# Moving the low-half subtractions of 32 quarters from VectorE to GpSimd in a decoder block

## The chip, the core and the metric

One core of a Trainium2 chip runs the whole kernel. The metric is the device time of one execution in microseconds (us). The engines are named as the profile names them: PE is TensorE's matmul, PEld its weight load, DVE is VectorE, ACT is ScalarE, POOL is GpSimd, SP is SyncE, which here only issues DMAs.

## What is computed

A decoder block over 1024 tokens of width 1024, in float32: attention with a sliding window beside a convolution, then an expert layer. This case is about the expert layer, which takes more than the last two thirds of the time:

```
q = (xb @ w_q).reshape(T, PEER_HEADS, 2, PEER_QDIM // 2)
s = jnp.einsum('thpc,hpkc->thpk', q, sub_keys)
top_s, top_i = lax.top_k(s, PEER_TOPK)
cand = top_s[:, :, 0, :, None] + top_s[:, :, 1, None, :]
best_s, best_c = lax.top_k(cand.reshape(T, PEER_HEADS, PEER_TOPK * PEER_TOPK), PEER_TOPK)
ids = i1 * N_KEYS + i2
g = jax.nn.softmax(best_s, axis=-1)
ue, ve = u_tab[ids], v_tab[ids]
act = gelu(einsum('td,thkd->thk', xb, ue))
out = einsum('td' <- 'thk,thkd', g * act, ve)
```

Each token picks 128 of 16384 experts (8 heads of 16). U and V (`u_tab`, `v_tab`) are 16384 x 1024 each.

## The kernel before, in words

The expert layer splits the tokens in halves of four 128-token tiles. The **first product** multiplies the tokens of tiles 1 to 3 of the lower half with all rows of U and writes the results to DRAM (`hidden`), from which the picked ones are read later; those of tile 0 are made one by one, as **dots** of a token with its gathered rows of U. A **second stage** treats the upper half densely (x times U, gelu, gates, times V) while the picked rows of V are gathered and summed for the lower half.

The first product runs over 128 **quarters**. Four quarters are a block of 512 experts; a quarter is two of the eight 128-row slices of the contraction. Float32 is made of two parts in the type fp32r, a high half that is the rounded value and a low half that is the rest. For each quarter Q:

- SP loads 512 KB of U into slot Q % 4 of `xraw` (`load_x`, L398), once the low half of quarter Q - 4 is made.
- ACT casts it to the high half `hx` (`high_u`, L822; the cast is L831), once TensorE has read the slot's old contents.
- The low half is `lx = xraw - hx`, one `tensor_tensor` of 128 x 1024 float32 (`low_wide`, L1237; L1240). Before the change VectorE makes all 128 of them.
- TensorE waits for the low half (L1793) and does 18 matmuls of 128 x 512 (L1801), six for each of three token tiles.
- After the fourth quarter of a block ACT copies three results to `hst` (`evict`, L854) and SP stores them (L417).

Around this, VectorE's program is one list in order (L1420 to L1434). At quarter Q it makes the low half first, then a share of the **picks**, then the marks, then the dots. The picks choose the 16 best experts per head of each of the eight token tiles, in 14 steps a tile (`pick`, L1250): sums of candidates (step 0), `max`, `max_index` and `match_replace` (steps 1 to 5), digits, ranks, 0/1 tables and their reductions (steps 6 to 13). Five tiles, 70 steps, are spread over quarters 4 to 35, 2.2 steps a quarter; the other three tiles over quarters 36 to 121. **Marks** (L1352) are 0/1 tables of 8 tokens of the upper half; from them POOL makes a scaled copy (`scale_hot`, L549) and ACT a plain one (L885), and TensorE multiplies the two in a **hot block** of 8 matmuls (L1787): two hot blocks in every three quarters from quarter 21 on. POOL's program (L595 to L601) does `scale_hot(n)` one quarter ahead of its hot block, and from quarter 39 on gathers the rows of U for the dots (L577; VectorE, L1409).

Three waits couple the engines besides: ACT takes the exponential of a tile's best scores (L858), in its own order behind the cast of a later quarter, and waits there for VectorE's step 6 (`best_ready`); TensorE transposes a tile's picks (L1777) after quarters 17, 24, 30 and 36 and waits for VectorE's step 13; step 10 on VectorE waits for the exponential.

Of the kernel before, what the change touches and what calls it, by code (L numbers as in the profile page):

```python
# [55 lines left out]
QB = DK // KQ  # L56
# [3 lines left out]
QUARTERS = QB * NB  # L60
FIRST_PICKS = 1 + HT
FIRST_QUARTERS = 36
LAST_PICK = QUARTERS - 6
X_BLOCK = FIRST_QUARTERS // QB - 1
X_QUARTER = FIRST_QUARTERS + 4
DOT_FROM = X_QUARTER + 1
# [15 lines left out]
VR = 2  # L82
# [30 lines left out]
F32 = mybir.dt.float32  # L113
# [3 lines left out]
ALU = mybir.AluOpType  # L117
# [5 lines left out]
def picks_done(Q):  # L123
    first = FIRST_PICKS * STEPS_PICK
    if Q < FIRST_QUARTERS:
        return first * max(0, Q + 1 - QB) // (FIRST_QUARTERS - QB)
    return min(NT * STEPS_PICK, first + (NT * STEPS_PICK - first) * (Q + 1 - FIRST_QUARTERS) // (LAST_PICK - FIRST_QUARTERS))


def query_place(m, half):  # L130

    return (1, 3, 2, 4)[2 * m + half] if m < 2 else 2 * m + half + 1


def quarter_of_step(k):
# [3 lines left out]
def stores(slot):  # L139
    return len(range(slot, (NB - 1) * PT, HSLOTS))  # L140
# [6 lines left out]
def hot_quarter(n):  # L147
    return 21 + n * 3 // 2
# [18 lines left out]
def decoder_block(nc, x, xT, w_in, w_out, w_q, keysT, uT, uX, u_tab, v_tab, ffn_g, consts, params, final_g, out):  # L167
# [15 lines left out]
    def at(offset, name, shape, dt=F32):  # L183

        with ExitStack() as there:
            if offset:
                there.enter_context(nc.sbuf_tensor(f"below_{name}", [P, offset // 4], F32))
            return there.enter_context(nc.sbuf_tensor(name, shape, dt))

    def sem(name):  # L190
        return ctx.enter_context(nc.semaphore(name))

    with ctx:
# [49 lines left out]
        xraw = at(HN, "xraw", [P, QB, KQ, WIDTH])  # L243
        hst = at(HN + 16384, "hst", [P, HSLOTS, WIDTH])
        hx = [at(offset, f"hx{r}", [P, KQ, WIDTH], F32R)
              for r, offset in enumerate((HN + 24576, HN + 28672, MID + 8192, MID + 12288))]
        lx = [at(MID + offset, f"lx{r}", [P, KQ, WIDTH], F32R)
              for r, offset in enumerate((82400, 86496, 123360, 127456))]
# [68 lines left out]
        def sems(names):  # L317
            return [sem(n) for n in names.split()]
# [16 lines left out]
        q_ready, q_copied, ks_ready, ks_free, wqh_ready, wql_ready = sems("q_ready q_copied ks_ready ks_free wqh_ready wql_ready")  # L335
        xraw_in = [sem(f"xraw_in{r}") for r in range(QB)]
        hx_ready, lx_ready, x_used, h1_ready, h1_free = sems("hx_ready lx_ready x_used h1_ready h1_free")
        hst_out = [sem(f"hst_out{n}") for n in range(HSLOTS)]
        best_ready, exp_ready, sel_ready, selT_ps, selT_ready = sems("best_ready exp_ready sel_ready selT_ps selT_ready")
        ids_ready = sem("ids_ready")  # L340
# [29 lines left out]
        def _(sp):  # L370
# [26 lines left out]

            def load_x(Q):  # L398
                if Q >= QB:
                    sp.wait_ge(lx_ready, Q - QB + 1)  # L400
                else:
                    sp.wait_ge(xl_ready, 2 * DK)
                b, r = divmod(Q, QB)
                sp.dma_start(xraw[:, r, :, :], uX[b, r]).then_inc(xraw_in[r], 16)

            def load_gates(g):
                sp.dma_start(gt[:, :, :, :], gates[g]).then_inc(g_in, 16)

            def store_hidden(B):
                for n in range(PT):  # L410
                    e = B * PT + n
                    sp.wait_ge(h1_free, e + 1)
                    dst = hidden[n * P:(n + 1) * P, B * WIDTH:(B + 1) * WIDTH]
                    if B == NB - 1:
                        sp.dma_start(dst, hlast[:, n, :]).then_inc(hlast_out, 16)
                    else:
                        sp.dma_start(dst, hst[:, e % HSLOTS, :]).then_inc(hst_out[e % HSLOTS], 16)  # L417
# [14 lines left out]
            for B in range(NB):  # L432
                for Q in range(QB * (B + 1) + 3, min(QB * (B + 2) + 3, QUARTERS)):
                    load_x(Q)
                if B == 0:
                    sp.dma_start(x_rows[0], xh[1][:, :, :].bitcast(F32)).then_inc(x_out, 16)
                    sp.dma_start(x_rows[1], xl[1][:, :, :].bitcast(F32)).then_inc(x_out, 16)
                if B == X_BLOCK:

                    sp.wait_ge(rows_out, 16)  # L440
                    sp.wait_ge(sel_ready, FIRST_PICKS)
                    sp.dma_start(uring[1][:, :], h_rows[:, 0, :]).then_inc(xt_in, 16)
                    sp.dma_start(uring[2][:, :], ffn_g.partition_broadcast(P)).then_inc(xt_in, 16)
                if B == NB - 1:
                    for c in range(2):
                        sp.wait_ge(lx_ready, QUARTERS - QB + c + 1)
                        sp.dma_start(u_raw[:, c, :], uT[c]).then_inc(u_in[c], 16)

                    for slot in range(HSLOTS):
                        sp.wait_ge(hst_out[slot], 16 * stores(slot))  # L450
                    load_gates(0)
                store_hidden(B)
                if B == hot_quarter(HT * BLOCKS - 1) // QB + 1:
                    for b in range(2):
                        sp.wait_ge(gates_out[b], 16 * (HALF // SUB // 2))
                    sp.wait_ge(hot_scaled, HT * BLOCKS + RAW)
                    sp.dma_start(xh[1][:, :, :].bitcast(F32), x_rows[0]).then_inc(x_back, 16)
                    sp.dma_start(xl[1][:, :, :].bitcast(F32), x_rows[1]).then_inc(x_back, 16)
                    sp.wait_ge(gp_ready, HT * BLOCKS * HQ + ROWS_CREDIT)
# [8 lines left out]
            def load_group(g, first=False):  # L468
                for c in range(GC):
                    n = g * GC + c  # L470
                    if n + 2 < NKEY:
                        sp.wait_ge(uh_ready, n + 1)
                        sp.wait_ge(ul_ready, n + 1)
                        sp.dma_start(u_raw[:, n % 2, :], uT[n + 2]).then_inc(u_in[n % 2], 16)
                    if not first or c >= VR:
                        sp.wait_ge(vh_ready, n - VR + 1)
                        sp.wait_ge(vl_ready, n - VR + 1)
                    sp.dma_start(v_raw[:, c % VR, :], v_tab[n]).then_inc(v_in[c], 16)
                    if c == 1 and not first:
                        sp.wait_ge(w_ready, g * GC)  # L480
                        load_gates(g)

            for c in range(VR):
                sp.wait_ge(lx_ready, QUARTERS - VR + c + 1)
            load_group(0, first=True)
            load_rows(1)
            load_rows(0)
# [11 lines left out]
        def _(pool):  # L499
# [91 lines left out]
                    in_offset=bass.IndirectOffsetOnAxis(ap=idsA[:, n, k:k + 1], axis=0)).then_inc(v_got[q % VS], 16)  # L591


            pool.sem_inc(hot_scaled, RAW)
            for Q in range(QUARTERS):  # L595
                for n in range(HT * BLOCKS):
                    if hot_quarter(n) - 1 == Q:
                        scale_hot(n)
                for k in range(P):
                    if quarter_of_dot(k) - 2 == Q:  # L600
                        gather_dot(k)  # L601
# [383 lines left out]
        def _(dve):  # L985
# [432 lines left out]

            marked = 0
            for Q in range(QUARTERS):  # L1420
                if Q >= QB:
                    low_wide(Q)
                picked(Q)
                if Q == X_QUARTER:
                    normed_rows()
                while marked < HT * BLOCKS and hot_quarter(marked) - 3 <= Q:
                    if marked == 0:
                        dve.drain()
                        dve.wait_ge(rows_out, 16)
                        dve.wait_ge(x_out, 32)  # L1430
                    mark(*divmod(marked, BLOCKS))
                    marked += 1
                for k in range(dots_done(Q - 1) if Q else 0, dots_done(Q)):
                    dot(k)  # L1434
# [55 lines left out]
        def _(pe):  # L1490
# [299 lines left out]

            def hidden_quarter(Q):
                B, quarter = divmod(Q, QB)
                pe.wait_ge(lx_ready, Q + 1)  # L1793
                for n in range(PT):
                    e, t0 = B * PT + n, (n + 1) * P
                    if quarter == 0 and e >= HSLOTS:
                        pe.wait_ge(h1_free, e - HSLOTS + 1)
                    for kk in range(KQ):
                        k = quarter * KQ + kk
                        for w, u in ((xh[0], hx), (xh[0], lx), (xl[0], hx)):  # L1800
                            last = mm(ps[:, e % HSLOTS, :], w[:, k, t0:t0 + P], u[quarter][:, kk, :],  # L1801
                                      start=k == 0 and w is xh[0] and u is hx, stop=k == DK - 1 and w is xl[0])
                    if quarter == QB - 1:
                        last.then_inc(h1_ready, 1)
                if quarter < QB - 1:
                    last.then_inc(x_used, 1)
                for n in range(HT * BLOCKS):
                    if hot_quarter(n) == Q:
                        hot_block(n)
# [130 lines left out]
```

## Time and profile before

| | us |
|---|---|
| median of 3 runs (lowest to highest) | 2835.77 (2834.06 to 2838.0) |
| profiled execution, whole | 2834.67 |
| its span, first to last instruction | 2832.7 |
| mean granted TensorE clock | 0.985 of full |

Busy shares of the span: PE 97%, DVE 80%, POOL 53%, ACT 37%. Busy time is that of instructions on an engine; a wait is the engine's idle time, put down to what ended it. In a timeline a row is start, duration, engine, line, operation, out<-in, shape and a count; the duration of a VectorE or GpSimd instruction runs from where the engine took it up to its end, so that neighbours can overlap by 0.1 us or so and a time in which the instruction could not get at its data is part of its duration.

### The profile page before, as it was taken

Reading aid. Unit: us, or ns where it says so; the run is one execution under the profiler, and the core shown is the slowest. Engines: PE = TensorE matmul, PEld = TensorE weight load, DVE = VectorE, ACT = ScalarE, POOL = GpSimd, SP = SyncE. Lnnn points to the kernel's source line nnn. Section 1 sums busy time; section 2 is a strip of 40 time slices with the busy share of each in tenths; the row PEclk is TensorE's granted clock in tenths of the full one; section 3 lists DMA queues with packets and bytes.
Section 4 is the critical chain, followed back from the end, with each engine's and each line's share of the span. In section 5 each row is a group of like instructions: output and inputs, shape, how many; then the busy total and the mean of one; then the engine's idle time right before and its main releaser. Section 6 shows DMA issues by size and latency. Waiting matters only on the chain.

```text
span 2832.7 us, 33409 instructions
## 1 busy us (share of the span) xinstructions
PE 2744.7 (97%) x11792; PEld 2098.8 (74%) x11792; DVE 2276.5 (80%) x3815; ACT 1034.6 (37%) x1374; POOL 1495.7 (53%) x1194
## 2 busy tenths in 40 slices
PE   8999699999899999999899999999999999999998
PEld 3444345888777888888778888888888888888886
DVE  1985533688998898888588889888989888898986
ACT  4443523211346656666323232232322323223233
POOL 3892100111023656665367777777777777777630
PEclk9989899999999999999999999999999999999999
DMA  5110100212546999999999898888989889888983
GB/s 194 45 45 1 60 15 23 75 46 84 203 149 220 323 329 345 335 348 344 373 358 330 300 328 306 314 315 306 327 298 327 301 312 327 301 326 299 342 302 137
DMA packets 254838, 687.75 MB, mean 243 GB/s; under 512 B 32080, under 2 KB 97744, under 8 KB 249168
## 3 DMA queue, kind: packets, MB, share of 16 engines
q0 software_dynamic: 104448, 335.81, 33.6%
q1 hardware_dynamic: 84432, 316.27, 30.9%
q10 hardware_dynamic: 65792, 33.56, 4.2%
q8 instruction: 93, 1.52, 0.2%
q14 instruction: 73, 0.60, 0.1%
HBM read 614.22 MB, written 71.30 MB: 242 GB/s over the span
## 4 chain that ended last, share of the span: by engine, by line
PE 71%; DVE 12%; DMA 7%; POOL 4%; DVEq 2%; issue 2%; ACT 1%; ACTq 0%; POOLq 0%; SPq 0%
PE ps L1836 24%; PE ps L1828 24%; PE ps L1801 6%; PE ps L1749 6%; DMA vring<-in_u_tab,idsA 5%; PE ps L1619 4%; DVE ps L1021 2%; POOL hnT L526 2%; PE ps L1787 1%; DVE lx L1240 1%; DVE vring L1409 1%; PE ps L1526 1%; POOL vring L577 1%; PE ps L1614 1%; DVE marks L1352 1%
## 5 line engine op out<-in xcount | busy, mean ns | idle before, releaser
L589 POOL DMA_INDIRECT vring<-in_v_tab,idsA x512 | 554.1, 1082 | 306.3 <-DVE ps L1392 162.7
L1392 DVE SCALAR_TENSOR_TENSOR ps<-vring,hsel,ps 128x1024 f32<-128x1024 f32 x508 | 652.7, 1285 | 29.4 <-DMA vring<-in_v_tab,idsA 11.7
L564 POOL DMA_INDIRECT hsel<-hidden,idsE x384 | 411.6, 1072 | 125.7 <-issue 106.4
L1836 PE MATMUL ps<-vh,wh 128*128 128x512 f32 x1024 | 401.9, 392 | 4.2 <-DVE acc L1469 4.2
L1836 PE MATMUL ps<-vh,wl 128*128 128x512 f32 x1024 | 405.9, 396 | 0.0
L1828 PE MATMUL ps<-xh,ul 128*128 128x512 f32 x1024 | 404.3, 395 | 0.0
L1828 PE MATMUL ps<-xh,uh 128*128 128x512 f32 x1024 | 403.4, 394 | 0.7 <-ACT hlast L854 0.7
L1828 PE MATMUL ps<-xl,uh 128*128 128x512 f32 x1024 | 402.4, 393 | 0.0
L1836 PE MATMUL ps<-vl,wh 128*128 128x512 f32 x1024 | 402.3, 393 | 0.0
L950 ACT CAST vh<-v_raw 128x1024 fp32r<-128x1024 f32 x128 | 134.1, 1047 | 585.5 <-PE ps L1836 580.0
L1801 PE MATMUL ps<-hx,xh 128*128 128x512 f32 x768 | 312.8, 407 | 29.0 <-DVE lx L1240 25.1
L1801 PE MATMUL ps<-lx,xh 128*128 128x512 f32 x768 | 308.7, 402 | 0.0
L1801 PE MATMUL ps<-hx,xl 128*128 128x512 f32 x768 | 306.9, 400 | 0.0
L577 POOL DMA_INDIRECT vring<-in_u_tab,idsA x128 | 181.1, 1414 | 161.9 <-DVE vring L1409 148.2
L549 POOL TENSOR_TENSOR hot<-marks,selG 128x1024 f32<-128x1024 bf16 x64 | 133.0, 2078 | 222.1 <-DVE marks L1352 127.3
L1836 PEld LDWEIGHTS ps<-vh,wh 128*128 128x128 f32 x1024 | 192.5, 188 | 49.1 <-DVE acc L1469 5.5
L831 ACT CAST hx<-xraw 128x1024 fp32r<-128x1024 f32 x128 | 134.1, 1049 | 256.7 <-PE ps L1801 166.1
L1836 PEld LDWEIGHTS ps<-vl,wh 128*128 128x128 f32 x1024 | 192.5, 188 | 47.0
L1828 PEld LDWEIGHTS ps<-xl,uh 128*128 128x128 f32 x1024 | 192.1, 188 | 46.3
L1828 PEld LDWEIGHTS ps<-xh,uh 128*128 128x128 f32 x1024 | 192.7, 188 | 45.0 <-ACT hlast L854 1.1
L1828 PEld LDWEIGHTS ps<-xh,ul 128*128 128x128 f32 x1024 | 192.3, 188 | 45.1
L1836 PEld LDWEIGHTS ps<-vh,wl 128*128 128x128 f32 x1024 | 192.4, 188 | 43.3
(197 smaller groups left out, 4707.6 us busy)
## 6 DMA issues: line engine op xcount, KB each, us to landing
xraw<-in_uX SPq DMA_DIRECT2D x128, 512.0 KB, 6.1
u_raw<-in_uT SPq DMA_DIRECT2D x128, 512.0 KB, 6.3
v_raw<-in_v_tab SPq DMA_DIRECT2D x128, 512.0 KB, 7.1
gates<-gbuf ACTq DMA_DIRECT2D x16, 2048.0 KB, 22.5
gt<-gates SPq DMA_DIRECT2D x32, 1024.0 KB, 9.0
hidden<-hst SPq DMA_DIRECT2D x93, 256.0 KB, 8.5
wbuf<-in_w_in SPq DMA_DIRECT2D x19, 512.0 KB, 3.6
wqbuf<-in_w_q SPq DMA_DIRECT2D x16, 512.0 KB, 3.5
```

The costliest lines, as they stand in the source:

```text
L549: nc.gpsimd.tensor_tensor(hot[:, b % ROWS, 1, :, :].rearrange("p (c e) k -> p c e k", e=2), marks[:, b % RAW, 1, :, :, :].rearrange("p c k ...
L564: nc.gpsimd.indirect_dma_start(out=hsel[:, n, k:k + 1], out_offset=None, in_=hidden_items, in_offset=bass.IndirectOffsetOnAxis(ap=idsE[:, ...
L577: nc.gpsimd.indirect_dma_start(out=uring[k % US][:, :], out_offset=None, in_=u_rows, in_offset=bass.IndirectOffsetOnAxis(ap=idsA[:, 0, k:k ...
L589: nc.gpsimd.indirect_dma_start(out=vring[q % VS][:, :], out_offset=None, in_=v_rows, in_offset=bass.IndirectOffsetOnAxis(ap=idsA[:, n, k:k ...
L831: nc.scalar.copy(hx[r][:, :, :], xraw[:, r, :, :]).then_inc(hx_ready, 1)
L950: nc.scalar.copy(vh[:, c, :], v_raw[:, c % VR, :]).then_inc(vh_ready, 1)
L1392: nc.vector.scalar_tensor_tensor(out=bank2(6), in0=vring[slot][:, :], scalar=w, in1=bank2(6), op0=ALU.mult, op1=ALU.add).then_inc(cb_done, 1)
L1619: last = mm(ps[:, bank, :], hnT[:, m, n * P:(n + 1) * P], wide[:, m, halfs(hb)], start=m == m0, stop=m == m0 + 3)
L1749: last = mm(ps[:, 2 * (m % 2) + half, :], w[:, m % 2, k, :], xx[:, k, :], start=k == 0 and xx is xh[half] and w is wqh, stop=k == DK - 1 a ...
L1801: last = mm(ps[:, e % HSLOTS, :], w[:, k, t0:t0 + P], u[quarter][:, kk, :], start=k == 0 and w is xh[0] and u is hx, stop=k == DK - 1 and ...
L1828: last = mm(ps[:, c % 2, :], w[n % USLOTS][:, k, :], xx[:, k, :], start=k == 0 and w is uh and xx is xh[1], stop=k == DK - 1 and w is ul)
L1836: last = mm(ps[:, 2 + k % 4, :], w[:, c, tt * P:(tt + 1) * P], v[:, c, dh * 512:(dh + 1) * 512], start=c == 0 and w is wh and v is vh, sto ...
```

## The change

GpSimd makes the low halves of quarters 4 to 35 (`LOW_POOL`), VectorE those of quarters 0 to 3 and 36 to 127. The subtraction is the same, on the same tiles. A second semaphore, `lx_pool`, counts GpSimd's; SP's loads, TensorE's quarters and the later loads wait for the count of whichever engine makes the low half. In POOL's program the subtraction of quarter Q comes before the `scale_hot` of that place in the list.

```
+LOW_POOL = range(QB, FIRST_QUARTERS)
+def lows_vector(Q):
+    return sum(q not in LOW_POOL for q in range(Q + 1))
+def lows_pool(Q):
+    return sum(q in LOW_POOL for q in range(Q + 1))
@@ SP, load_x
-                    sp.wait_ge(lx_ready, Q - QB + 1)
+                    if Q - QB in LOW_POOL:
+                        sp.wait_ge(lx_pool, lows_pool(Q - QB))
+                    else:
+                        sp.wait_ge(lx_ready, lows_vector(Q - QB))
@@ GpSimd
+            def low_wide(Q):
+                r = Q % QB
+                pool.wait_ge(hx_ready, Q + 1)
+                nc.gpsimd.tensor_tensor(lx[r][:, :, :], xraw[:, r, :, :], hx[r][:, :, :].bitcast(F32),
+                                        ALU.subtract).then_inc(lx_pool, 1)
             for Q in range(QUARTERS):
+                if Q in LOW_POOL:
+                    low_wide(Q)
                 for n in range(HT * BLOCKS):
                     if hot_quarter(n) - 1 == Q:
                         scale_hot(n)
@@ VectorE
-                if Q >= QB:
+                if Q >= QB and Q not in LOW_POOL:
                     low_wide(Q)
@@ TensorE, hidden_quarter
-                pe.wait_ge(lx_ready, Q + 1)
+                if Q in LOW_POOL:
+                    pe.wait_ge(lx_pool, lows_pool(Q))
+                else:
+                    pe.wait_ge(lx_ready, lows_vector(Q))
```

## Rows read from the trace of the kernel before

**Rows 1.** Busy time by stage: busy us (count), PE clock, DMA share, GB/s.

```profile
718.00:893.00 175.00, 161.60 (x745) 131.94 (x745) 167.00 (x487) 79.25 (x99) 27.85 (x12) 0.95 0.55 181
893.00:1393.00 500.00, 486.97 (x2524) 410.61 (x2524) 414.04 (x677) 293.93 (x339) 287.60 (x181) 0.99 0.97 338
1393.00:2833.00 1440.00, 1424.91 (x6144) 1154.04 (x6144) 1257.63 (x1327) 415.78 (x556) 964.33 (x895) 1.00 0.87 309
```

**Rows 2.** Waits in 718 to 893: total us, times, longest us.

```profile
POOL hot L549 <- DVE marks L1352: 127.0, 3, 117.5
...
ACT hx L831 <- PE ps L1801: 60.8, 19, 9.6
...
PE ps L1801 <- DVE lx L1240: 12.3, 8, 4.0
ACT best L858 <- DVE best L1279: 9.7, 3, 4.0
```

**Rows 3.** VectorE's timeline: low halves of quarters 0 and 1, 4, 36.

```profile
692.27 2.35 DVE L1240 TENSOR_TENSOR lx<-xraw,hx 128x1024 fp32r<-128x1024 f32 x2
...
718.09 1.22 DVE L1240 TENSOR_TENSOR lx<-xraw,hx 128x1024 fp32r<-128x1024 f32 x1
...
893.20 1.22 DVE L1240 TENSOR_TENSOR lx<-xraw,hx 128x1024 fp32r<-128x1024 f32 x1
```

**Rows 4.** TensorE's timeline: end of quarter 3, first matmuls of quarters 4 and 36.

```profile
715.00 0.39 PE L1801 MATMUL ps<-hx,xl 128*128 128x512 f32 x1
719.37 0.79 PE L1801 MATMUL ps<-hx,xh 128*128 128x512 f32 x1 [3.98 <-DVE lx L1240]
...
894.47 0.50 PE L1801 MATMUL ps<-hx,xh 128*128 128x512 f32 x1 [1.64 <-DVE lx L1240]
```

**Rows 5.** The chain in 1164 to 1192: a quarter and a hot block alone.

```profile
1182.07 4.16 PE ps L1801 x18
1186.23 1.78 PE ps L1787 x16
```

**Rows 6.** VectorE's groups in 718 to 893, shapes apart: count, busy us, mean ns.

```profile
L1240 DVE TENSOR_TENSOR lx<-xraw,hx 128x1024 fp32r<-128x1024 f32 x32 | 38.9, 1216 | 0.0
...
L1274 DVE FIND_INDEX8 bpos<-best,cand 128x8 uint32<-128x112 f32 x40 | 9.9, 271 | 0.0
...
L1270 DVE MAX8 best<-cand 128x8 f32<-128x112 f32 x40 | 7.6, 261 | 0.4
```

**Rows 7.** Two lines of GpSimd over the span: ns min/median/max, first and last start.

```profile
L540 POOL TENSOR_TENSOR wql<-wqbuf,wqh x16: 2355/2385/2399, 412.1 to 669.4; 128x1024 fp32r<-128x1024 f32 x16
...
L549 POOL TENSOR_TENSOR hot<-marks,selG x64: 1892/1910/2962, 789.3 to 1318.4; 128x1024 f32<-128x1024 bf16 x64
```

**Rows 8.** GpSimd's timeline in 786 to 893: four of its twelve instructions.

```profile
796.99 2.81 POOL L549 TENSOR_TENSOR hot<-marks,selG 128x1024 f32<-128x1024 bf16 x1 [4.88 <-DVE marks L1352]
...
827.27 1.90 POOL L549 TENSOR_TENSOR hot<-marks,selG 128x1024 f32<-128x1024 bf16 x1 [8.01 <-PE ps L1787]
...
882.21 2.28 POOL L549 TENSOR_TENSOR hot<-marks,selG 128x1024 f32<-128x1024 bf16 x1 [9.22 <-PE ps L1787]
888.16 1.90 POOL L549 TENSOR_TENSOR hot<-marks,selG 128x1024 f32<-128x1024 bf16 x1 [3.67 <-PE ps L1787]
```

**Rows 9.** VectorE's timeline beside those four.

```profile
796.82 1.22 DVE L1240 TENSOR_TENSOR lx<-xraw,hx 128x1024 fp32r<-128x1024 f32 x1
798.13 1.81 DVE L1292 SCALAR_TENSOR_TENSOR ranks<-bdig 128x128 bf16<-128x128 f32 x1
799.87 0.28 DVE L1294 SCALAR_TENSOR_TENSOR ranks<-bdig 128x128 bf16<-128x128 f32 x1
...
827.76 0.26 DVE L1266 MATCH_REPLACE8 cand<-best,cand 128x112 f32<-128x112 f32 x1
...
881.51 4.06 DVE L1311 TENSOR_TENSOR picks<-picks,i16p 128x2048 bf16<-128x2048 bf16 x2
...
888.40 1.81 DVE L1323 TENSOR_TENSOR sel<-best,den 128x128 f32<-128x128 f32 x1
```

**Rows 10.** Busy time by stage around quarter 4, columns as in rows 1.

```profile
719.00:725.00 6.00, 5.63 (x13) 4.46 (x14) 5.75 (x26) 0.00 (x0) 0.00 (x0) 0.50 0.38 111
```

More of the change, by code:

```diff
@@ L337, in decoder_block @@
         hx_ready, lx_ready, x_used, h1_ready, h1_free = sems("hx_ready lx_ready x_used h1_ready h1_free")
+        lx_pool = sem("lx_pool")
         hst_out = [sem(f"hst_out{n}") for n in range(HSLOTS)]
@@ L445, in _ @@
                     for c in range(2):
-                        sp.wait_ge(lx_ready, QUARTERS - QB + c + 1)
+                        sp.wait_ge(lx_ready, lows_vector(QUARTERS - QB + c))
                         sp.dma_start(u_raw[:, c, :], uT[c]).then_inc(u_in[c], 16)
@@ L483, in _ @@
             for c in range(VR):
-                sp.wait_ge(lx_ready, QUARTERS - VR + c + 1)
+                sp.wait_ge(lx_ready, lows_vector(QUARTERS - VR + c))
             load_group(0, first=True)
```

## The prediction

> **What bounds the kernel now.** I read the busy time by stage first. The first product runs from about 697 to 1393 us, the second stage behind it. From 893 on TensorE is busy 487.0 of 500 us and then 1424.9 of 1440 [rows 1]: what starts earlier or later there starts so as a whole, and keeps its length. The stretch 718 to 893, quarters 4 to 35, is another matter: VectorE is busy 167.0 of 175 us, TensorE 161.6 [rows 1]. There the change works.
>
> Next the waits of that stretch. TensorE waits for a low half 8 times, 12.3 us in all, and ACT three times, 9.7 us, for the best scores of VectorE's step 6 [rows 2]. At both ends TensorE starts just behind VectorE: quarter 4's low half starts at 718.09 and its matmul at 719.37, quarter 36's at 893.20 and 894.47 [rows 3, 4]. So quarters 4 to 35 last 175.1 us on either engine, and VectorE, with its picks, marks and low halves in one list, sets this.
>
> What would TensorE need alone? A quarter is 4.16 us, a hot block 1.78 [rows 5]. Quarters 4 to 20 make 17 x 4.16 = 70.7; 21 to 35 have two hot blocks in three quarters, 15 x 4.16 + 10 x 1.78 = 80.2; together 151 us.
>
> **What is taken from VectorE.** 32 instructions of 1.22 us [rows 6]. They overlap their neighbours a little: two in a row take 2.35 [rows 3], so one is worth 1.13 and 32 are worth 36.2. Left are 175.1 - 36.2 = 138.9 us, if nothing else changed.
>
> **What is put on GpSimd.** 32 `tensor_tensor` of the same shape and types as L540's, 2.385 us each, against 1.91 for L549's [rows 7]: 32 x 2.385 = 76.3 us, beside 12 of L549, 22.9 us net. POOL was busy 27.85 of 175 [rows 1], so it has the time. In its queue each low half stands ahead of the `scale_hot` of its place, and the next low half behind that: behind it TensorE's next quarter and SP's load of the slot wait. `scale_hot` waits for VectorE's mark (127.0 us, of which 117.5 before the first [rows 2]); a mark stands three places ahead of its hot block in VectorE's list, so low halves from quarter 21 on can't run more than two places ahead of VectorE. The counting semaphores add one instruction to no engine. No DMA is added; `load_x` and the stores behind it in SP's queue follow the low halves as before.
>
> **What the move does to VectorE.** This term decides, and the trace shows it at twelve places, the twelve L549 of the stretch. At 796.99 GpSimd takes one up while VectorE does a low half (796.82, 1.22): GpSimd's lasts 2.81 where 1.90 is the usual, up to 799.80, and VectorE's next, L1292, lasts 1.81 where its like take 0.28 [rows 8, 9]. It ends 0.14 behind GpSimd's. At 882.21 it falls between two products of bf16 tables: GpSimd's lasts 2.28, and the two, 1.22 each elsewhere, last 4.06 [rows 8, 9]. So each waits until the other's instruction is through. It isn't so with `max`, `max_index` and `match_replace`: at 827.27 GpSimd takes its 1.90 and L1266 beside it stays at 0.26 [rows 8, 9]. Nine of the twelve held up a VectorE instruction in this way, by 1.5 (L1292 at 798.13, the first), 1.7, 1.7, 1.5, 1.1, 1.5, 0.6, 1.7 and 1.5 us (L1323 at 888.40, the last) [rows 9]: 12.9 us in all. The Trainium skill says why, in SBUF — State Buffer, "Who interferes with whom": GpSimd shares a port pair with VectorE, and an instruction with two SBUF inputs, or a copy in a two-port mode, and one of GpSimd's shut each other out whole. The trace agrees (4.06 against 2 x 1.22). [...]
>
> **The sum for VectorE.** Its own work in the stretch is 138.9 - 12.9 = 126 us. Of this the kinds that GpSimd doesn't touch are five groups of 40 (`max_index` and `match_replace` three times 9.8 to 9.9 busy, `max` twice 7.6: 44.8 [rows 6]) and the gaps and small reductions between them, about 50; the others, which shut out GpSimd and are shut out, 76. GpSimd's work is 76.3 + 22.9 = 99 us; the low halves of quarters 4 to 6 can run before 718, beside VectorE's scans, so 92 fall into the stretch. VectorE then needs 126 + 92 x (1 - c), where c is the share of GpSimd's time that falls on the 50 us.
> - c can't be over 50 / 92 = 0.54: 168 us, 7 less than now. With c = 0 it is 218, 43 more.
> - By chance alone c would be 50 / 126 = 0.40: 181 us, 6 more. The twelve rows give 1 - 12.9 / 22.9 = 0.44: 178, 3 more.
> - But GpSimd's times aren't left to chance. With 181 us for 32 quarters VectorE takes 5.6 us a quarter, TensorE 4.16 up to quarter 20 and 5.35 after. TensorE and ACT run ahead until ACT stands at the exponential and waits for step 6, which it does now three times in five [rows 2]. VectorE's `max` and `match_replace` steps, 1 to 5, fall into that wait, and no cast comes out, so no work for GpSimd. When step 6 is done ACT casts two or three quarters in a row and GpSimd subtracts them one behind the other, through VectorE's steps 6 to 13, which are of the kind that it shuts out, and between two of its own it lets one of VectorE's in. I take c = 0.25: one hold in four beside the untouched steps, about 2 of the 9 or so holds of a tile's picks. 126 + 69 = 195 us, **20 more**.
>
> **The end of the stretch.** Quarter 36's low half is VectorE's again, behind all 70 steps, so it moves from 893.2 to about 913. TensorE is done with quarter 35 some us before (5 to 8, as TensorE is the faster and quarter 4 starts at 715.2, right behind quarter 3, not at 719.37 [rows 4]) and stands. After the 4 us of waiting before quarter 4 its granted clock was 0.5, 1.2 GHz, for about 6 us [rows 10]; that cost 2.7 us in the quarter. I add 2 for the same at quarter 36. From there the list is as before, at TensorE's pace: 22 us later to the end. 2834.67 + 22 = 2856.7, **2857 us**. The profiled execution is 1.1 under the median of the three runs; I add nothing for that.
>
> **Rivals.**
> - *TensorE becomes the bound* (faster). If GpSimd's subtraction didn't hold up VectorE, VectorE would need 126 + 12.9 = 139 us, TensorE 151 from 715.2: quarter 36 at 866 instead of 894.5, 28 less, 2807 us. It decides if the hold is under (151 - 126) / 44 = 0.6 us for each of the 44 instructions. For it: POOL's idle time. Against: nine of twelve held up VectorE by more.
> - *The holds fall as by chance* (no change). c of 0.38 to 0.54: 7 less to 8 more, 2828 to 2843, if TensorE and ACT don't stand at step 6. For it: the twelve rows give 0.44. Against: these follow TensorE's hot blocks, not ACT's casts.
> - *Nearly every hold hits* (slower still). c under 0.12: 33 to 43 more, and 2 for the clock: 2870 to 2880.
>
> **How the numbers follow.** Chances: forecast (c of 0.12 to 0.38, 8 to 33 more, with the 2: 2845 to 2870) 0.66; by chance 0.17; TensorE bound 0.09; nearly every hold 0.08. Two tenths of a percent, what a measurement of this kernel can tell from no change, are 5.7 us. Faster by more: the TensorE rival and the edge of the second, 0.10. Within: most of the second, 0.12. Slower: the forecast, the rest of the second and the third, 0.78. The range 2835 to 2873 leaves out the first rival, the faster half of the second and most of the third's, 0.19.
>
> **What would show it.** In the new trace: 32 `lx` on POOL of 2.4 us or, where they wait first, up to 3.6; VectorE's two-input and copy instructions between 718 and quarter 36 longer by some 70 us in sum, the `max` kind unchanged; ACT's waits for step 6 five times in five, over 25 us; quarter 36's low half near 913; TensorE waiting over 4 us before it. After it the same lengths as before. Wrong would be: low halves on GpSimd and VectorE's durations unchanged (then the first rival), or the sum of holds near 50 (the second).

## The result and the profile after

The changed kernel takes **2854.06 us** (median of five runs, 2847.48 to 2855.29) against 2834.56 us of the kernel before, run beside it (2833.49 to 2838.0): a ratio of 1.006, 95% interval 1.0049 to 1.0071. By the medians it is 19.5 us slower, by the ratio 17 (14 to 20); 22 were forecast (2857 us, range 2835 to 2873). The profiled execution spans 2853.0 us, 20.3 more than before, at a granted clock of 0.983.

The same stages as in [rows 1], moved by what they come later (columns: busy us and count of PE, PEld, DVE, ACT, POOL; PE clock, DMA share, GB/s):

```profile
697.00:718.00 21.00, 19.84 (x94) 16.12 (x94) 20.10 (x118) 7.28 (x9) 8.07 (x3) 1.00 0.46 147
718.00:893.00 175.00, 150.27 (x673) 121.46 (x671) 168.43 (x450) 66.57 (x86) 91.60 (x39) 0.93 0.46 154
893.00:914.00 21.00, 17.69 (x80) 14.85 (x81) 20.22 (x22) 13.51 (x16) 3.79 (x2) 0.85 0.61 195
914.00:1414.00 500.00, 485.74 (x2519) 409.21 (x2518) 413.47 (x672) 292.95 (x337) 285.67 (x181) 0.99 0.97 338
1414.00:2853.00 1439.00, 1424.18 (x6140) 1154.36 (x6138) 1256.64 (x1327) 415.73 (x556) 964.28 (x895) 1.00 0.87 309
```

From 914 on the busy times are nearly those of before, some 20 us later. The stretch of quarters 4 to 35 has grown from 175 to some 190 us, so that it isn't over at 893. In the 175 us shown VectorE is as full as before (168.43), although the 32 low halves are gone from its list: it gets through 450 instructions instead of 487. POOL's busy time there has gone from 27.85 to 91.60.

VectorE's timeline at both ends of the stretch, and TensorE's at quarter 36, which answer to [rows 3] and [rows 4] (start, duration, engine, line, operation; in brackets the wait ahead):

```profile
719.52 1.68 DVE L1256 CAST i16p<-i 128x256 bf16<-128x256 uint32 x1
721.28 1.16 DVE L1276 TENSOR_TENSOR cand<-s 128x512 f32<-128x512 f32 x2
...
908.79 1.22 DVE L1261 TENSOR_TENSOR lx<-xraw,hx 128x1024 fp32r<-128x1024 f32 x1
```

```profile
906.91 0.39 PE L1825 MATMUL ps<-hx,xl 128*128 128x512 f32 x1
910.06 0.50 PE L1825 MATMUL ps<-hx,xh 128*128 128x512 f32 x1 [2.76 <-DVE lx L1261]
```

The scans end 1.6 us later than before (717.88), as quarter 0 of the first product, ahead of all that is changed, starts 1.6 us later too (698.62 instead of 696.99). That isn't the change's doing: in the traces of the experiments quarter 0 starts between 0.9 us earlier and 2.7 later than in that of before, whatever the kernel. The cast behind the scans lasts 1.68, as GpSimd does a low half from 718.65 to 721.05, and the picks run from 721.28 to 908.79. Quarter 36's low half starts 15.6 us later than before (893.20), and TensorE goes on with it, as it did before.

VectorE's groups between 718 and 909, shapes apart (count | busy us, mean ns | idle), some that grew and two that did not:

```profile
L1332 DVE TENSOR_TENSOR picks<-picks,i16p 128x2048 bf16<-128x2048 bf16 x10 | 17.8, 1820 | 0.4
...
L1322 DVE TENSOR_TENSOR picks<-ranks,iota 128x2048 bf16<-128x2048 bf16 x10 | 16.2, 1665 | 0.4
L1352 DVE TENSOR_TENSOR picks<-picks 128x2048 bf16<-128x2048 bf16 x5 | 9.9, 1985 | 0.4
L1295 DVE FIND_INDEX8 bpos<-best,cand 128x8 uint32<-128x112 f32 x40 | 9.9, 270 | 0.3 <-issue 0.3
...
L1307 DVE TENSOR_SCALAR bdig<-bpos 128x128 uint32<-128x128 uint32 x25 | 8.3, 395 | 0.0
...
L1291 DVE MAX8 best<-cand 128x8 f32<-128x112 f32 x40 | 7.6, 262 | 0.4
```

L1332, L1322 and L1352 take 1.22 us each where GpSimd is idle; here the means are 1.82, 1.67 and 1.99. `max_index` (L1295) and `max` (L1291) last what they lasted in [rows 6]. A *hold* is what a VectorE instruction lasts beyond the usual of its shape, counted from 0.1 us on. Added up from 718 to quarter 36, the holds are 63.7 us in 34 instructions, instead of 12.9 in 9. Sorted by the GpSimd instruction that each falls on, 50.2 us in 26 are the low halves' and 13.5 in 8 `scale_hot`'s.

One of the places: GpSimd's timeline and VectorE's, just after VectorE's step 6 has let ACT go on.

```profile
770.60 7.12 POOL L610 TENSOR_TENSOR lx<-xraw,hx 128x1024 fp32r<-128x1024 f32 x3 [12.18 <-ACT hx L852]
778.71 2.74 POOL L610 TENSOR_TENSOR lx<-xraw,hx 128x1024 fp32r<-128x1024 f32 x1 [0.98 <-ACT hx L852]
```

```profile
770.66 2.45 DVE L1313 SCALAR_TENSOR_TENSOR ranks<-bdig 128x128 bf16<-128x128 f32 x1
773.03 2.47 DVE L1315 SCALAR_TENSOR_TENSOR ranks<-bdig 128x128 bf16<-128x128 f32 x1
775.57 2.31 DVE L1318 TENSOR_TENSOR ranks<-ranks,bdig 128x128 bf16<-128x128 bf16 x1
777.95 4.58 DVE L1322 TENSOR_TENSOR picks<-ranks,iota 128x2048 bf16<-128x2048 bf16 x2
```

These are three low halves behind one another, and each holds up one VectorE instruction of 0.29 us until it is through; between two of GpSimd's, exactly one of VectorE's gets in here. The fourth low half, at 778.71, falls between the two of L1322: 4.58 instead of 2.44.

The waits between 718 and 909 (total, times, longest), which answer to [rows 2]:

```profile
ACT best L879 <- DVE best L1300: 36.6, 5, 13.3
POOL lx L610 <- ACT hx L852: 29.5, 11, 12.2
...
PE ps L1798 <- DVE sel L1352: 10.6, 2, 6.9
...
PE ps L1825 <- ACT hst L875: 8.6, 4, 3.2
```

ACT now waits for step 6 five times in five, 36.6 us instead of 9.7. TensorE waits little for low halves now (2.7 us for GpSimd's, and 2.76 before quarter 36), but for a tile's picks (`sel`, 10.6) and for ACT to copy its results out (8.6).

### The profile page after: what moved, and what is told of

It is laid out like the page before. It is cut to its first block, busy times and chain, and to the rows that moved or that the text cites. A ratio compares the mean times of both kernels' runs of the same rounds, so it can differ in the third digit from the quotient of the medians.

```text
span 2853.0 us, 33409 instructions
## 1 busy us (share of the span) xinstructions
PE 2749.9 (96%) x11792; PEld 2103.0 (74%) x11792; DVE 2295.3 (80%) x3783; ACT 1033.7 (36%) x1374; POOL 1569.3 (55%) x1226
## 4 chain that ended last, share of the span: by engine, by line
PE 66%; DVE 14%; DMA 8%; POOL 4%; DVEq 3%; issue 3%; ACT 1%; ACTq 0%; POOLq 0%; SPq 0%
PE ps L1860 24%; PE ps L1852 24%; DMA vring<-in_u_tab,idsA 7%; PE ps L1770 6%; PE ps L1640 4%; DVE ps L1042 2%; PE ps L1825 2%; POOL hnT L539 2%; DVE vring L1430 2%; DVE marks L1373 1%; POOL vring L590 1%; PE ps L1547 1%; DVE lx L1261 1%; PE ps L1635 1%; POOL hot L562 1%
## 5 line engine op out<-in xcount | busy, mean ns | idle before, releaser
L553 POOL TENSOR_TENSOR wql<-wqbuf,wqh 128x1024 fp32r<-128x1024 f32 x16 | 38.1, 2382 | 326.3 <-ACT wqh L813 326.3
```

## The experiments

Times are given against runs of the kernel before on the same chip.

### GpSimd reads and writes something idle

Two kernels leave all low halves on VectorE, as before the change, and give GpSimd work that nobody needs, in the places of the 32 low halves and not before the scans are done: 32 subtractions of a constant tile from itself, or 64 fills. Nothing of the computation is left out. `swork` is free by then.

```
 # the kernel before, and in GpSimd's program at quarters 4 to 35:
+    pool.wait_ge(hx_ready, Q + 1)
+    ...                                                                   # quarter 4 waits for the scans, too
+    nc.gpsimd.tensor_tensor(swork[:, :, :], fixed, fixed, ALU.subtract)   # first kernel
+    2 x nc.gpsimd.memset(swork[:, :, :], 0.0)                             # second kernel
```

> The kernel before, with VectorE keeping all low halves, and 32 subtractions of a constant tile from itself added on GpSimd, 128 x 1024 float32, into a tile that is free by then; each waits for the cast of quarter 4 to 35 as the change's low halves do. Nobody waits for them. Theory (an instruction of GpSimd's that reads SBUF shuts out VectorE's two-input and copy instructions whole): VectorE's own work in the stretch is 162 us with its low halves, of which 50 are untouched; 32 x 2.4 = 77 us of holds, 0.69 of them on the rest: 45 to 60 us slower than before. Rival (the change lost its time by order: the low halves stand in GpSimd's queue behind scale_hot and the marks, and ACT behind step 6): these subtractions release nobody, so within 5 us of before.

> As e1_idle_reads, but two fills of the free tile with zeros (GpSimd memset of 128 x 1024 float32, no input) at each of the 32 places, so that GpSimd is occupied at the same moments and reads nothing. Theory (VectorE's second input is what is shut out, so GpSimd has to read): within 6 us of before. Rival (any instruction of GpSimd's shuts VectorE out for its length, or GpSimd's occupation delays scale_hot): 20 us slower or more, as the fills are about as long as a subtraction.

The subtractions: 2871.47 us, one execution, 36.8 more (the 15 of the kernel before lie between 2830.68 and 2838.66); in the trace of this execution quarter 36 comes 36.4 us later, and 25 holds, 35.2 us, fall on the subtractions. The fills: 2837.65 (ten runs), a ratio of 1.0014, interval 1.0004 to 1.0023, 3 more. GpSimd's group and three of VectorE's with the subtractions, in 718 to 893 for VectorE and up to 931 for GpSimd:

```profile
L602 POOL TENSOR_TENSOR swork<-con 128x1024 f32<-128x1024 f32 x32 | 65.1, 2034 | 94.9 <-DVE i16p L1247 46.6 <-ACT hx L843 45.3 <-issue 1.6
```

```profile
L1254 DVE TENSOR_TENSOR lx<-xraw,hx 128x1024 fp32r<-128x1024 f32 x27 | 38.6, 1429 | 0.0
...
L1345 DVE TENSOR_TENSOR sel<-picks 128x256 f32<-128x256 bf16 x4 | 6.3, 1584 | 0.3
...
L1284 DVE MAX8 best<-cand 128x8 f32<-128x112 f32 x32 | 6.0, 261 | 0.3
```

and the same with the fills:

```profile
L602 POOL MEMSET swork<- 128x1024 f32 x64 | 61.3, 959 | 85.3 <-DVE i16p L1247 46.6 <-ACT hx L843 32.5
```

```profile
L1254 DVE TENSOR_TENSOR lx<-xraw,hx 128x1024 fp32r<-128x1024 f32 x31 | 37.7, 1216 | 0.0
...
L1315 DVE TENSOR_TENSOR picks<-ranks,iota 128x2048 bf16<-128x2048 bf16 x10 | 11.8, 1222 | 0.4
...
L1300 DVE TENSOR_SCALAR bdig<-bpos 128x128 uint32<-128x128 uint32 x25 | 8.2, 548 | 0.0
```

GpSimd is busy about as long in both (65.1 and 61.3 us). Nothing waits for its results in either, and no transfer is added, so what the first costs more it costs by being there. Beside the subtractions VectorE's two-input instructions grow (L1254 to 1.43 in the mean, and nearly four times its 0.43 for L1345), and `max` stays. Beside the fills the two-input ones keep their length (1.22 for L1254 and L1315): some 50 of them meet a fill, and the only ones that stand, six, stand at a `scale_hot`. So it is GpSimd's reading that holds the two-input instructions up; the rival that gave the first kernel within 5 us falls, and so does the one that gave the fills 20 or more. The size of the first was missed: 45 to 60 was expected, 36.8 came. The idle subtraction lasts 1.9 us where nothing is in its way, not the 2.4 of a low half (it reads one tile twice; whether that is the reason isn't shown): 32 x 1.9 = 61 us, and 36.8 / 61 = 0.6 us of delay for each us of GpSimd, which for 32 x 2.4 would have been 46.

### GpSimd copies something idle

The same with one operand read.

```
-    nc.gpsimd.tensor_tensor(swork[:, :, :], fixed, fixed, ALU.subtract)
+    nc.gpsimd.tensor_copy(swork[:, :, :], fixed)
```

> The kernel before plus 32 idle copies on GpSimd (one operand read, one written, 128x1024 float32), in the places in which the run with idle two-operand subtractions had those (+36.8 us for 32 of 1.9 us), and the run with 64 idle fills had its fills (+3 for 64 of 0.95 us). This leaves out nothing of the computation. Theory (what shuts VectorE out is that GpSimd reads through the shared ports, however many operands): each holds by its length, so about as much per us of GpSimd: +15 to +37, by its duration (1 to 1.9 us each). Rival (it takes two operands read): as the fills, under +6.

2849.03 us against 2836.2, a ratio of 1.0046, interval 1.003 to 1.0061: 12.8 more.

```profile
L602 POOL COPY swork<-con 128x1024 f32<-128x1024 f32 x32 | 38.5, 1203 | 99.2 <-ACT hx L843 50.0 <-DVE i16p L1247 46.6
```

Two of the copies, and VectorE beside them:

```profile
806.74 2.27 POOL L602 COPY swork<-con 128x1024 f32<-128x1024 f32 x2
```

```profile
807.02 0.97 DVE L1311 TENSOR_TENSOR ranks<-ranks,bdig 128x128 bf16<-128x128 bf16 x1
808.06 3.16 DVE L1315 TENSOR_TENSOR picks<-ranks,iota 128x2048 bf16<-128x2048 bf16 x2
```

L1311, 0.29 us elsewhere, lasts 0.97, and the two L1315 last 3.16 instead of 2.44, where beside the fills no two-input instruction stood at a fill. The rival (under 6) falls: one operand read is enough to hold VectorE. The price is 2 us under the bound given, 12.8 / 38.5 = 0.33 us per us that GpSimd is busy, against 36.8 / 65.1 = 0.57 for the subtractions. A part of the difference is that a hold is shorter than the GpSimd instruction that it falls on, and more so, for its length, at a short one: 23 holds of 0.7 us on average at copies of 1.2, 25 of 1.4 at subtractions of 2.0. Another part lies behind the stretch: quarter 36 is 16.6 us later in the trace, the end 14.9. The rest was not pursued.

### The same number of low halves, beside two kinds of VectorE work

These two settle the term on which the forecast rests, *where* the low halves fall. Both give GpSimd 16 of them, quarter 4's and three for each tile of picks. In the first, GpSimd waits for a tile's step 0 and then works beside steps 1 to 5 (`max`, `max_index`, `match_replace`); in the second it waits for step 6's last instruction and works beside the tables of steps 7 to 9.

```
-LOW_POOL = range(QB, FIRST_QUARTERS)
+LOW_BESIDE = ((5, 6, 7), (11, 12, 13), (18, 19, 20), (24, 25, 26), (31, 32, 33))   # beside max
+LOW_BESIDE = ((8, 9, 10), (14, 15, 16), (20, 21, 22), (27, 28, 29), (33, 34, 35))  # beside tables
+LOW_POOL = (4, *(Q for p in LOW_BESIDE for Q in p),)
@@ GpSimd, low_wide, for the three quarters of tile p
+    pool.wait_ge(pick_at, p + 2)
@@ VectorE: the semaphore is raised by step 0's last instruction (max) or by step 6's (tables)
```

> GpSimd makes 16 low halves: quarter 4's beside the scans, and for each of the five tiles three quarters' low halves that wait, besides for the cast, until the tile's step 0 is done, so that they start with steps 1 to 5 (max, max_index, match_replace): quarters 5 to 7, 11 to 13, 18 to 20, 24 to 26, 31 to 33. Theory (it matters beside which of VectorE's instructions GpSimd works): 3 x 2.4 = 7.2 us fit into the 9 us of these steps, VectorE loses 16 x 1.13 = 18 us of work and gets few new holds, TensorE starts quarter 4 without its 4 us wait: 10 to 16 us faster than before. Rival (what counts is how many low halves GpSimd makes, since each costs some 2 us of holds for 1.13 saved, in the change 0.55 us net a quarter): 16 x 0.55 = 9 us slower.

> The counterpart of e6_beside_max: also 16 low halves, quarter 4's and three for each of five tiles, but these wait until the tile's step 6 is done, so that they start with steps 7 to 9 (ranks and 0/1 tables, two inputs each): quarters 8 to 10, 14 to 16, 20 to 22, 27 to 29, 33 to 35. Theory: nearly every one of the 15 holds VectorE by about 2.2 us, 33 us for 18 saved: 12 to 25 us slower than before. Rival (number, not place): 9 us slower, the same as e6_beside_max.

Beside `max`: 2821.76 us, a ratio of 0.9952, interval 0.9939 to 0.9966, **12.9 us faster** than the kernel before. Beside the tables: 2852.08, 1.0061, interval 1.0045 to 1.0076, 17.4 slower. The same engine does the same work, 30 us apart. VectorE's two groups behind step 6, first beside `max`, then beside the tables:

```profile
L1328 DVE TENSOR_TENSOR picks<-ranks,iota 128x2048 bf16<-128x2048 bf16 x10 | 13.4, 1385 | 0.4
...
L1321 DVE SCALAR_TENSOR_TENSOR ranks<-bdig 128x128 bf16<-128x128 f32 x5 | 1.4, 284 | 0.0
```

```profile
L1327 DVE TENSOR_TENSOR picks<-ranks,iota 128x2048 bf16<-128x2048 bf16 x10 | 28.1, 2844 | 0.4
L1320 DVE SCALAR_TENSOR_TENSOR ranks<-bdig 128x128 bf16<-128x128 f32 x5 | 11.9, 2385 | 0.0
...
L1312 DVE TENSOR_SCALAR bdig<-bpos 128x128 uint32<-128x128 uint32 x25 | 3.8, 220 | 0.0
```

The five instructions of 0.28 us become 2.39 each, a low half's length, and the ten products, 1.22 where nothing holds them, become 2.84. All in all the holds are 47.7 us there and 15.6 beside `max`. The 15 low halves of the stretch have 31.6 us of them beside the tables, in 40 us of GpSimd's time, and 1.8 beside `max`, in 37 us; the rest falls on the 12 `scale_hot`, which alone had 12.9 before.

Beside `max` the gain up to quarter 36 is still less than what VectorE saves. 16 x 1.13 = 18 are off its list, 15.6 - 12.9 = 2.7 are lost to holds, and 15.4 should be left, but quarter 36's low half starts only 9.6 us earlier in the trace:

```profile
883.56 1.22 DVE L1266 TENSOR_TENSOR lx<-xraw,hx 128x1024 fp32r<-128x1024 f32 x1
```

The waits of VectorE show most of the difference:

```profile
DVE marks L1379 <- ACT selG L890: 5.5, 1, 5.5
```

The first marks need a tile that TensorE transposes and ACT copies in their own order, and VectorE now arrives there 5.5 us too early (1.0 before). At the end this trace is 13.1 us shorter than that of before; 4.3 of that come between quarters 55 and 87, where ten of the eleven other traces, this one among them, gain 0.7 to 4.7 us on that of before, whatever the kernel.

### More low halves beside max

> As the run that starts three low halves of each tile behind step 0 (16 quarters, 2821.8 us beside 2834.7), but with four for the first three tiles and the last two tiles' three one quarter earlier: 19 quarters of GpSimd. Theory: three more instructions of 1.13 are off VectorE's list, 3.4 us; a fourth behind step 0 begins some 7 us after it, when steps 1 to 5 (10 to 12 us) still run, and costs little: 3 to 5 us under the run with 16, a ratio to the kernel before of 0.993 to 0.995. Rival (a fourth doesn't fit beside the untouched steps and is held): the same as with 16 or up to 3 more, 0.995 to 0.997. Rival (TensorE is the bound already): the same as with 16.

```
+LOW_BESIDE = ((5, 6, 7, 8), (11, 12, 13, 14), (18, 19, 20, 21), (23, 24, 25), (30, 31, 32))
```

2819.21 us against 2836.2, a ratio of 0.9948, interval 0.9933 to 0.9962: 17 us faster than the kernel before, the lowest ratio here. Its interval overlaps that of the 16 low halves (0.9939 to 0.9966), so the times don't tell theory and rivals apart. In the traces the low halves have 4.3 us of holds here against 1.8, which is 2.5 of the 3.4 that three more of them save; quarter 36 starts 2.2 us earlier. VectorE's wait for `selG` is 5.5 us here, too.

### ACT's exponential two quarters later

The forecast chose c, the share of GpSimd's time that falls beside VectorE's untouched steps, under the chance value of 0.40, because ACT stands at the exponential and lets no cast out while VectorE does these steps. This kernel is the change, with that wait two casts later in ACT's list.

```
-                    if quarter_of_step(p * STEPS_PICK + 6) == Q - 3:
+                    if quarter_of_step(p * STEPS_PICK + 6) == Q - 5:
```

> The change as it is (GpSimd makes quarters 4 to 35), but ACT takes each exponential two quarters later in its list (two casts more stand ahead of it). Theory of the prediction: ACT stands at the exponential while VectorE does max and match_replace, no cast comes out, and GpSimd then subtracts beside the picks' tables, which is why fewer of its instructions than by chance meet VectorE's max kind. With two casts more ahead of the wait GpSimd gets work in these steps: 3 to 6 us less of holds, ACT's waits for step 6 under 15 us in all instead of 36.6, and 2847 to 2852 against 2854.1. Rival (the share of holds has nothing to do with ACT's wait): ACT waits less, the time stays at 2853 to 2856. Rival (step 10 now waits for the exponential): 2857 or more.

2846.02 us against 2832.99, a ratio of 1.0045, interval 1.0028 to 1.0062: 13.0 more than before where the change costs 19.5. Its waits between 718 and 903:

```profile
PE ps L1798 <- DVE sel L1352: 9.3, 2, 7.2
...
PE ps L1825 <- POOL lx L610: 6.8, 2, 4.3
...
ACT best L879 <- DVE best L1300: 5.7, 2, 4.9
```

ACT waits 5.7 us for step 6 instead of 36.6, and VectorE's holds fall from 63.7 to 59.4. That is the direction and the size expected (3 to 6 us); the time is 1 us under the range given. Both rivals (2853 and more, a ratio of at least 1.0065) fall just outside the interval. In the traces GpSimd works beside the untouched steps for 24 of its 97 us here, and for 20 of its 96 in the change, so ACT's wait does keep low halves away from these steps. But it is a small part of the matter: they take 46 of VectorE's 125 us of own work, so by chance it would be over a third of GpSimd's time, and without the wait it is a quarter. What else keeps the low halves away was not pursued. How much of the change's cost the wait makes isn't told either: 13.0 stands beside 19.5, but the intervals overlap (1.0028 to 1.0062 and 1.0049 to 1.0071), and of the 6.8 us by which quarter 36 comes earlier in this trace, 2.5 are there at quarter 0. Most of the cost is there without the wait.

### Half of the quarters, and three of them

```
-LOW_POOL = range(QB, FIRST_QUARTERS)      # the change
+LOW_POOL = range(QB, 20)                  # first half
+LOW_POOL = range(20, FIRST_QUARTERS)      # second half
+LOW_POOL = (4, 5, 6)                      # beside the scans
```

> GpSimd makes the low halves of quarters 4 to 19 only, VectorE all others. There is hardly a hot block in these quarters, so beside the picks' steps VectorE has little else, and TensorE needs only 4.16 us a quarter. Theory (holds): 16 x 1.13 = 18 us are taken from VectorE; GpSimd works 16 x 2.4 = 38 us, of which some 7 before quarter 4, and VectorE stands for 0.7 of the other 31, 22 us: 4 more, and 2 more if TensorE stands before a quarter that VectorE sets. 2837 to 2845 beside 2834.7 of the kernel before. Rival (the cost is spread evenly over the 32): half of the change's, +10, 2844 to 2846. Rival (the cost comes from the hot blocks and marks alone, behind quarter 20): 18 us are gained here, of which TensorE's own pace lets some 10 through, 2820 to 2828.

> GpSimd makes the low halves of quarters 20 to 35 only, VectorE all others. Here GpSimd also scales 12 blocks of marks and VectorE makes the marks. Theory (holds): 18 us are taken from VectorE, GpSimd works 16 x 2.4 = 38 us, none of it ahead of the stretch, and VectorE stands for 0.7 to 0.8 of it, 27 to 30 us: 9 to 12 more, and 2 for the slow quarter behind TensorE's wait before quarter 36: 2844 to 2850. Together with the first half's run this should give about the +17 to +20 of the whole change. Rival (even spread): +10, 2844 to 2846. Rival (only the first half costs): under +3.

> GpSimd makes the low halves of quarters 4, 5 and 6 only, VectorE all others. In the change's own trace these three start between 697 and 720 us, beside VectorE's scans and not beside picks. Theory: 3 x 1.13 = 3.4 us are taken from VectorE, with hardly a hold against it, and TensorE starts quarter 4 right behind quarter 3, so that its wait of 4 us and the slow quarter behind it (2.7 us) are gone, which helps only as far as VectorE's own list comes earlier: 2829 to 2832. Rival (a low half on GpSimd costs VectorE the same wherever it stands, 20 / 32 = 0.6 us each): 2836 to 2838. Rival (the front of the stretch doesn't count): 2834 to 2835.5.

First half: 2838.76 against 2832.99, ratio 1.0017 (1.0007 to 1.0028), 5.8 more. Second half: 2845.3, 1.0039 (1.0025 to 1.0053), 12.3 more. Together they make 18.1, about the change's 19.5. Both are as the theory had them. The even spread falls with the first half (+10 would be a ratio of 1.0035) and is not told apart by the second; that hot blocks and marks alone are to blame falls as well, since the first half has next to none and is not faster; that only the first half costs (under 3 more with the second) falls by the second's 12.3. The second half is dearer by its holds, 39.6 us against 33.8 in the first: 26.2 fall on its 16 low halves, all beside picks, and 21.7 on the first half's, three of which come before 718, as in the change (8.07 us of POOL in its row for 697 to 718).

Those three alone: 2831.86, ratio 0.9994, interval 0.9984 to 1.0003. That a low half costs the same wherever it stands (2836 to 2838 beside 2834.7, at least 1.0005) falls just outside; whether three of them beside the scans gain 3 us or nothing can't be told.

## Why the prediction came out right

- **What bounds the kernel.** Right: quarter 36 again starts behind VectorE's low half, and all behind it came later as a whole.
- **What is taken from VectorE, and its own work.** 126 us were forecast for VectorE without low halves and holds. From 721.28 to 908.79 are 187.5 us; less the 62.3 of holds in them, 125.2 are left.
- **GpSimd's work.** 2.385 us were forecast for a low half, up to 3.6 where it waits. The trace has a median of 2.40 and a maximum of 3.38. 29 of them and 12 of `scale_hot` (22.8 us) lie between 718 and quarter 36: 96 us, not 92; the 4 are the low halves' own waits.
- **The holds.** 69 us were forecast, 63.7 measured. The mechanism is as told: GpSimd's instruction holds VectorE's, one VectorE instruction gets in between two, and `max`, `max_index` and `match_replace` are untouched (GpSimd overlaps 92 of some 200, and none is over 0.3 us). The share c = 0.25 was an estimate, and as the sum uses it, 1 - 63.7 / 96, it is 0.34. But c was meant as GpSimd's time beside the untouched steps, and that is 20 of 96 us, 0.21; 34 of GpSimd's 41 instructions hold something up, where three in four were forecast. What was too high is the price of one: the sum took a hold to be as long as GpSimd's instruction, 2.35 us on average, and a hold is 1.9. So the share came near, and two errors, too few holds and too long ones, partly cancel. That ACT's wait pushes the share down was right in direction (20 us against 24 without the wait), but it is not the main reason why it lies under chance.
- **Quarter 36's low half.** Near 913 was forecast, 908.79 measured: 5 us fewer of holds, against a start that lay 1.6 later.
- **The clock behind TensorE's wait.** TensorE was to wait 5 to 8 us before quarter 36, and 2 us were added for the slow matmuls behind that. It waited 2.76. What was overlooked is that TensorE is not free to run ahead: it transposes a tile's picks before quarters 18, 25 and 31 and waits twice there for VectorE's step 13 (10.6 us), and four times for its results to be copied out (8.6). That these waits alone bring it late to quarter 36 is not shown, as the next figures say. The clock fell all the same:

```profile
910.00:916.00 6.00, 5.94 (x19) 4.73 (x20) 5.91 (x8) 0.00 (x0) 0.00 (x0) 0.72 0.63 186
```

0.72 in the mean of these six us against 0.50 in [rows 10], where the wait had been 4 us. From quarter 36 to quarter 39 the delay grew from 15.6 to 17.2 us, 1.6 instead of 2. With the exponential two quarters later the wait before quarter 36 was 7.91, as forecast for the change, and the delay grew by 2.5, although TensorE waited nearly as long for step 13 (9.3).
- **Behind it.** "The same lengths as before" was right to 3 us. The delay is 17.2 us up to quarter 53, 19.2 at quarter 55, where ACT waits 4.5 us for a load of U, 18.1 from quarter 87 to 120, and 20.3 at the end. In some experiments it grows at quarter 55 too, by up to 1.2 us; none of them bears on why.
- **The rivals.** TensorE doesn't become the bound, since the hold is no 0.6 us for each instruction but 1.55 (63.7 / 41). The holds by chance, 42 to 57 us of them, are what the later exponential comes near to (59.4), and it is 13 us slower than before, 5 more than that rival's upper end, partly by the slow matmuls behind TensorE's 7.91 us of waiting. Nearly every hold hits in the kernel beside the tables: all of 15 low halves, 31.6 of their 40 us. In the change 26 of 29 do; the time stays under that rival's, as these have only 50.2 of the low halves' 73.4 us.

The total is closer than its terms by luck, as errors cancel: 5 us of holds too many stand against 1.6 us that were there before the first product and 3 that came behind quarter 39, neither of which the prediction or the change accounts for.

## What to carry to other kernels

An idle GpSimd is no free place for work beside a busy VectorE: price a moved instruction by what VectorE does in the same microseconds. Beside instructions that GpSimd doesn't hold up it is nearly free (2 us for 37 of GpSimd's), beside two-input ones it costs most of its own length (32 for 40), so that the same move is a gain or a loss by its place alone. To get the gain, let GpSimd's instruction wait for the start of such a stretch, and then look for who is early: here the marks' wait of 5.5 us was the largest that VectorE had left.

## What the runs showed of the hardware

Fills, which read nothing, held up another kind than the reading instructions. VectorE's two-input products kept 1.22 us beside 64 fills, but L1300, with one uint32 input, went to a mean of 548 ns, against 220 in the kernel beside the tables (its L1312), where GpSimd stands still during them. Sixteen holds, 10.8 us, fall on the fills, all of `tensor_scalar`, copies and casts; with those on `scale_hot` VectorE stood 23 us, 10 more than before, of which only 3 us reached the end. The Trainium skill has this in SBUF — State Buffer, "Who interferes with whom": a two-input VectorE instruction contends with a GpSimd instruction that reads, not with one that only writes, and `tensor_scalar`, `copy` and `cast` can take the shared pair. The traces agree on both. The prediction's wording left out that GpSimd's instruction has to read; both kinds that it dealt with, `scale_hot` and the low halves, do. Ports can't be seen in a trace; what is seen are these durations.

That ten us of holds cost only 3 in the fills' run was not expected either. Its trace is 7.0 us late at quarter 36 and 2.2 late between quarters 87 and 108. The five go between quarters 55 and 87, where nearly all the traces gain on that of before; so a few us at the end of one trace, against one of before, say little on what GpSimd did before quarter 36.
